# RMS norms that sum their squares as token columns, take the root there and spread it with four products

## The chip, the cores and the metric

The kernel runs on one core of one Trainium2 chip. A core has five engines that run side by side and meet at semaphores: PE (TensorE, matrix products), DVE (VectorE, elementwise), ACT (ScalarE, activation functions), POOL (GpSimd) and SP, which here issues DMAs. PE writes to PSUM only; the other tiles lie in SBUF, with 128 partitions. The metric is the device time of one execution in microseconds (us); lower is better.

## The reference

The program computes two transformer-like blocks on 512 tokens of width 1024 (with a context of 256 tokens, and a memory of 256 tokens), about fifty weight arrays in all, and a final norm. The change touches only the RMS norms over the model width:

```
def _rmsnorm(x, g):
    x32 = x.astype(jnp.float32)
    y = x32 * lax.rsqrt(jnp.mean(x32 * x32, axis=-1, keepdims=True) + EPS)
    return (y * g.astype(jnp.float32)).astype(x.dtype)
```

In the first block the same norm is followed by `modulate`, h * (1 + scale) + shift. The norms of query and key heads and of the gated linear attention are other code and stay as they are. Seven norms go through the changed code, in five stages:

```
h  = modulate(rms_norm(x, norm1_g[l]), shift1, scale1)      # stage 1, 512 tokens
hc = modulate(rms_norm(xc, norm1_g[l]), cmods[0], cmods[1]) # stage 1, 256 tokens, done first
h  = modulate(rms_norm(x, norm2_g[l]), shift2, scale2)      # stage 2, before the experts
mem_n = _rmsnorm(mem, g_mem); h = _rmsnorm(x, g_mix)        # stage 3, 256 and 512 tokens
hm = _rmsnorm(x, g_mlp)                                     # stage 4
return _rmsnorm(x, g_final)                                 # stage 5
```

## The kernel before, in words

Activations lie transposed: the model width is cut into KD = 8 tiles of P = 128 channels, one channel per partition, and the tokens run along the free dimension (n = 512 or 256 columns). The kernel is a row of stages. Each is a block in which every engine has its own list of instructions, written out by hand, and all engines meet at a barrier at the end of the block. So inside a norm stage nothing of the stage before or after runs, except weight loads that were issued earlier (and, in stage 1, the splitting of two weight chunks on ACT and POOL).

A norm stage (`norm_stage`, line 456) takes a list of items. For each item:

- ACT squares the eight tiles into a ring of four buffers `sq` (line 484), and waits for PE to have used a buffer before it is filled again.
- PE adds up over the partitions with a product (line 511). The stationary operand is `K.ones`, 128 x 128; the moving operand is the tile of squares with its n token columns. The eight products accumulate in one bank of PSUM, and since all of `K.ones` is one, every partition of the result holds the same row of n sums.
- DVE makes mean plus EPS out of it (line 530, n columns on every partition), then the reciprocal (line 532).
- ACT takes the root (line 489), n columns on every partition, into `rstd`.
- DVE multiplies each of the eight tiles by its gain column and by `rstd` (line 536). Where the output is split in two parts (`pair`), ACT writes the high part of each tile (lines 494 and 496), and DVE the rest (lines 521 and 523); otherwise ACT adds the shift (line 501), or nothing follows. In stage 5 SP stores each tile when it is scaled.

A float32 product shows in the trace as two records of the matrix product (PE) and two of the weight load (PEld): 16 records for eight products. Other products that are named below are `mod_turn` (line 319, stationary 128 x 128 and two moving columns), the router's (line 259 called from the stage behind stage 2: stationary 128 x 128, 16 moving columns), line 1254 of the gated linear attention (128 x 128 and 128 moving columns) and the transposes of line 2510. All these are float32 too.

Within a stage with two items PE's list is: eight products of the first item, a wait for the first item's mean (`mean_done`), eight products of the second.

Of the kernel before, what the change touches and what calls it, by code (L numbers as in the profile page):

```python
# [10 lines left out]
ACT = mybir.ActivationFunctionType  # L11
AX = mybir.AxisListType

P = 128
D = 1024
KD = D // P
S = 512
# [3 lines left out]
EPS = 1e-6  # L21
# [433 lines left out]

def norm_stage(K, items, tmp, store=None, split=None, first=()):

    sq_done, stored, mean_done, rec_done, rstd_done, scaled, shifted, sq_used, hi_done, lo_done = K.signals(10)
    sq = K.at(tmp, 4, S)
    rec, rstd = K.at(tmp + 8, S), K.at(tmp + 10, S)  # L460
    full = K.at(tmp + 12, KD, S) if any(isinstance(it[2], tuple) for it in items) else None
    with K.nc.Block() as block:
        @block.sync
        def _(sp):
            K.start(sp)
            if store is not None:
                for t in range(KD):
                    sp.wait_ge(scaled, t + 1)
                    sp.dma_start(store[t * P:(t + 1) * P, :], items[0][2][:, t, :]).then_inc(stored, 16)
                sp.wait_ge(stored, 16 * KD)  # L470

        @block.gpsimd
        def _(pool):
            for n in first:
                split.low(K, pool, n)

        @block.scalar
        def _(act):
            for j, (x, n, out, gain, shift) in enumerate(items):
                for t in range(KD):  # L480
                    a = j * KD + t
                    if a >= 4:
                        act.wait_ge(sq_used, a - 3)
                    act.activation(sq[:, a % 4, 0:n], x[:, t, :], ACT.Square).then_inc(sq_done, 1)  # L484
                if j == 0:
                    for c in first:
                        split.high(K, act, c)
                act.wait_ge(rec_done, j + 1)
                act.activation(rstd[:, 0:n], rec[:, 0:n], ACT.Sqrt).then_inc(rstd_done, 1)  # L489
                if isinstance(out, tuple):  # L490
                    for t in range(KD):
                        act.wait_ge(scaled, j * KD + t + 1)
                        if shift is None:
                            ins = act.activation(out[0][:, t, :], full[:, t, :], ACT.Copy)
                        else:
                            ins = act.activation(out[0][:, t, :], full[:, t, :], ACT.Identity, bias=shift(t))
                        ins.then_inc(hi_done, 1)
                elif shift is not None:
                    for t in range(KD):
                        act.wait_ge(scaled, j * KD + t + 1)  # L500
                        act.activation(out[:, t, :], out[:, t, :], ACT.Identity, bias=shift(t)).then_inc(shifted, 1)

        @block.tensor
        def _(pe):
            for j, (x, n, out, gain, shift) in enumerate(items):
                if j >= 1:
                    pe.wait_ge(mean_done, j)
                for t in range(KD):
                    a = j * KD + t
                    pe.wait_ge(sq_done, a + 1)  # L510
                    pe.matmul(K.ps[:, 0, 0:n], K.ones[:, :], sq[:, a % 4, 0:n], start=(t == 0), stop=(t == KD - 1))\  # L511
                        .then_inc(sq_used, 1)

        @block.vector
        def _(dve):
            for j, (x, n, out, gain, shift) in enumerate(items):
                def rest(t):
                    f, hi, lo = full[:, t, :], out[0][:, t, :].bitcast(F32), out[1][:, t, :]
                    dve.wait_ge(hi_done, t + 1)
                    if shift is None:  # L520
                        ins = dve.tensor_tensor(lo, f, hi, ALU.subtract)
                    else:
                        ins = dve.scalar_tensor_tensor(lo, f, shift(t), hi, ALU.add, ALU.subtract)
                    ins.then_inc(lo_done, 1)

                pair = isinstance(out, tuple)
                dve.wait_ge(sq_used, (j + 1) * KD)
                if j >= 1:
                    dve.wait_ge(scaled, j * KD)
                dve.tensor_scalar(rec[:, 0:n], K.ps[:, 0, 0:n], 1.0 / D, EPS, ALU.mult, ALU.add).then_inc(mean_done, 1)  # L530
                dve.wait_ge(mean_done, j + 1)
                dve.reciprocal(rec[:, 0:n], rec[:, 0:n]).then_inc(rec_done, 1)  # L532
                dve.wait_ge(rstd_done, j + 1)
                for t in range(KD):
                    dest = full[:, t, :] if pair else out[:, t, :]
                    dve.scalar_tensor_tensor(dest, x[:, t, :], gain(t), rstd[:, 0:n], ALU.mult, ALU.mult)\  # L536
                        .then_inc(scaled, 1)
                    if pair and t >= 2:
                        rest(t - 2)
                if pair:  # L540
                    rest(KD - 2)
                    rest(KD - 1)
            dve.wait_ge(scaled, len(items) * KD)
# [3175 lines left out]
def block2_stages(K):  # L3719
    K.memT, K.qd, K.kd, K.vd = K.at(72, KD, NCTX), K.at(72, 6, S), K.at(84, 6, S), K.at(96, 12, 256)  # L3720
    K.qm, K.kmT, K.vm = K.at(108, 4, S), K.at(116, 4, NCTX), K.at(120, 2, 512)
    K.rg = K.at(124, 2, 6, P)
    K.hank0, K.hank1, K.hank2 = K.at(124, 4, 256), K.at(128, 4, P), K.at(130, 4, P)
    K.lru_rate, K.flip, K.pick = K.at(132, 6), K.at(132.5, P), K.at(133, 256)[0:4]
    return [
        lambda: load_memory_stage(K),
        lambda: norm_stage(K, [(K.memT, NCTX, K.memT, gain_of(K, "g_mem_2"), None),
                               (K.xT, S, (K.h_hi, K.h_lo), gain_of(K, "g_mix_2"), None)], 80),
        lambda: memory_project_stage(K),
        lambda: lru_weights_stage(K),  # L3730
        lambda: lru_stage(K),
        lambda: dilated_project_stage(K),
    ]
# [16 lines left out]
def mlp_stages(K):  # L3750
    rounded_h(K)
    return [
        lambda: norm_stage(K, [(K.xT, S, (K.h_hi, K.h_lo), gain_of(K, "g_mlp_2"), None)], 128),
        lambda: mlp_stage(K),
    ]


def final_stages(K):
    K.hT = K.at(16, KD, S)
    return [  # L3760
        lambda: norm_stage(K, [(K.xT, S, K.hT, gain_of(K, "g_final_2"), None)], 72, store=K.out),
    ]
# [59 lines left out]
```

## Time and profile before

| | |
|---|---|
| median of 3 runs | 2583.42 us (2577.92 to 2586.68) |
| profiled execution | 2587.65 us, of which the span from first to last instruction is 2585.8 us |
| PE busy | 2220.1 us, 86% of the span |
| DVE busy | 1147.4 us, 44% |
| ACT busy | 866.6 us, 34% |
| mean granted TensorE clock | 0.912 of full speed |

Busy shares are averages over some forty stages with different limits. PE is the busiest engine of the whole, but a stage such as a norm, shut in between two barriers, is as long as its own chain: squares, products, mean, reciprocal, root, scaling. TensorE has two clock levels, 1.2 and 2.4 GHz; PEclk gives the granted one as a share of full speed, 0.50 for 1.2 GHz. In the first 45 us of the trace the column shows 1.00 while the records have the lengths of the lower level, so there lengths are to be read, not that column.

### The profile page before, as it was taken

What the parts mean: (1) busy time and instruction counts of PE and PEld (TensorE: products, weight loads), DVE (VectorE), ACT (ScalarE), POOL (GpSimd) and SP (SyncE); (2) the same over time, 40 slices, a digit from 0 to 9 for tenths busy, and PEclk for the clock granted to TensorE, in tenths of its full rate; (3) what the DMA queues carried; (4) which work ended last, traced back from release to release, by engine and by line L of the source; (5) the groups of instructions that cost most, each with busy time, mean ns of one, the idle gap of its engine ahead of it and who ended that gap; (6) DMA issues with size and microseconds to landing.
All of it is one profiled execution on the core that took longest, in us unless ns stands there. A gap on an engine that the chain in (4) does not pass through costs nothing. (4 is left out here: it accounts for less than half of the span.)

```text
span 2585.8 us, 23825 instructions
## 1 busy us (share of the span) xinstructions
PE 2220.1 (86%) x9452; PEld 1660.4 (64%) x9452; DVE 1147.4 (44%) x1486; ACT 866.6 (34%) x1124; POOL 576.9 (22%) x178
## 2 busy tenths in 40 slices
PE   5789987979888999759999637989779987999997
PEld 2667753547327887657777525678448865788885
DVE  1444357625654123247888543711761232322323
ACT  2441212323212222226777421831532232222221
POOL 0320110022113444010000101333014440544340
PEclk9896888989998999859999868999889998999999
DMA  6213022322004233139999802222012231323210
GB/s 209 88 65 134 24 83 98 131 81 78 0 0 130 74 98 106 49 131 354 376 383 388 316 19 87 98 80 85 11 31 92 90 106 49 130 75 104 81 66 33
DMA packets 174848, 299.69 MB, mean 116 GB/s; under 512 B 8943, under 2 KB 66490, under 8 KB 174744
## 3 DMA queue, kind: packets, MB, share of 16 engines
q1 hardware_dynamic: 169400, 279.93, 31.4%
q0 software_dynamic: 3040, 9.93, 1.1%
q10 hardware_dynamic: 2304, 8.39, 0.8%
q8 instruction: 72, 1.18, 0.2%
q14 instruction: 32, 0.26, 0.0%
HBM read 275.10 MB, written 23.13 MB: 115 GB/s over the span
## 5 line engine op out<-in xcount | busy, mean ns | idle before, releaser
L130 POOL TENSOR_TENSOR region<-weights,region 128x2048 fp32r<-128x2048 f32 (+2 forms) x96 | 378.6, 3945 | 1053.8 <-ACT region L124 917.6
L236 PE MATMUL ps<-region 128*128 128x512 f32 (+1 forms) x1336 | 538.2, 403 | 80.9 <-PEq L2743 16.6
L239 PE MATMUL ps<-region 128*128 128x512 f32 (+1 forms) x1336 | 524.8, 393 | 0.0
L240 PE MATMUL ps<-region 128*128 128x512 f32 (+1 forms) x1336 | 524.3, 392 | 0.0
L236 PEld LDWEIGHTS ps<-region 128*128 128x128 f32 x1336 | 263.1, 197 | 146.4 <-issue 44.7
L239 PEld LDWEIGHTS ps<-region 128*128 128x128 f32 x1336 | 263.0, 197 | 54.8 <-issue 5.4
L240 PEld LDWEIGHTS ps<-region 128*128 128x128 f32 x1336 | 262.1, 196 | 51.1
L124 ACT ACTIVATE region<-weights 128x2048 fp32r<-128x2048 f32 (+2 forms) x98 | 158.4, 1621 | 319.8 <-PE ps L240 278.6
L2584 DVE TENSOR_TENSOR region<-weights,region 128x2048 fp32r<-128x2048 f32 x96 | 218.7, 2290 | 67.0 <-ACT region L2523 66.8
L277 PE MATMUL ps<-region 128*128 128x512 f32 x512 | 203.8, 398 | 24.3 <-POOL region L3353 21.9
L2523 ACT ACTIVATE region<-weights 128x2048 fp32r<-128x2048 f32 x96 | 183.8, 1918 | 84.9 <-DMA weights<-moe_w_up 30.7
L3353 POOL TENSOR_TENSOR region<-weights,region 128x2048 fp32r<-128x2048 f32 x32 | 148.9, 4667 | 233.2 <-ACT region L3414 233.2
L279 PE MATMUL ps<-region 128*128 128x512 f32 x512 | 200.6, 392 | 0.0
L278 PE MATMUL ps<-region 128*128 128x512 f32 x512 | 200.1, 391 | 0.0
L2465 PE MATMUL ps<-region 128*128 128x512 f32 x384 | 154.5, 402 | 10.8 <-issue 8.6
L2195 DVE TENSOR_TENSOR region<-ps,region 128x512 f32<-128x512 f32 x48 | 33.1, 690 | 281.1 <-PE ps L240 281.1
L2467 PE MATMUL ps<-region 128*128 128x512 f32 x384 | 151.6, 395 | 0.0
L2466 PE MATMUL ps<-region 128*128 128x512 f32 x384 | 151.5, 395 | 0.0
L277 PEld LDWEIGHTS ps<-region 128*128 128x128 f32 x512 | 96.7, 189 | 47.6 <-POOL region L3353 22.8
L279 PEld LDWEIGHTS ps<-region 128*128 128x128 f32 x512 | 96.5, 189 | 20.8
L278 PEld LDWEIGHTS ps<-region 128*128 128x128 f32 x512 | 96.9, 189 | 19.3
L3414 ACT ACTIVATE region<-weights 128x2048 fp32r<-128x2048 f32 x32 | 60.1, 1910 | 119.8 <-PE ps L3394 118.4
(375 smaller groups left out, 2801.0 us busy)
## 6 DMA issues: line engine op xcount, KB each, us to landing
weights<-w_in SPq DMA_DIRECT2D x54, 1024.0 KB, 5.1
weights<-moe_w_gate SPq DMA_DIRECT2D x32, 1024.0 KB, 8.0
weights<-moe_w_up SPq DMA_DIRECT2D x32, 1024.0 KB, 8.9
weights<-moe_w_down SPq DMA_DIRECT2D x32, 1024.0 KB, 7.7
weights<-w_mod SPq DMA_DIRECT2D x24, 1024.0 KB, 5.2
weights<-w_mlp_in SPq DMA_DIRECT2D x16, 1024.0 KB, 5.1
weights<-w_mlp_out SPq DMA_DIRECT2D x16, 1024.0 KB, 5.0
h_slots<-region SPq DMA_DIRECT2D x16, 512.0 KB
```

Source lines behind the costliest of these rows:

```text
L124: act.activation(flat(self.part(K, n, 0)), flat(r.view(n)), ACT.Copy).then_inc(self.hi_done, 1)
L130: eng.tensor_tensor(flat(self.part(K, n, 1)), flat(self.ring.view(n)), flat(self.part(K, n, 0)).bitcast(F32), ALU.subtract).then_inc(self. ...
L236: ins = pe.matmul(out, l_hi, r_hi, start=(start and k == 0), stop=False)
L239: pe.matmul(out, l_hi, r_lo, start=False, stop=False)
L240: ins = pe.matmul(out, l_lo, r_hi, start=False, stop=(stop and k == kt - 1))
L277: pe.matmul(out, w_hi, x_hi, start=(n == 0), stop=False)
L278: pe.matmul(out, w_hi, x_lo, start=False, stop=False)
L279: last = pe.matmul(out, w_lo, x_hi, start=False, stop=(n == len(triples) - 1))
L2465: pe.matmul(K.ps[:, bank, :], x_hi[:, x, :], w_hi[:, k, :], start=(start and k == 0), stop=False)
L2467: ins = pe.matmul(K.ps[:, bank, :], x_lo[:, x, :], w_hi[:, k, :], start=False, stop=(stop and k == 3))
L2523: act.activation(flat(part(c, 0)), r.slots[n % RING][:, :], ACT.Copy).then_inc(hi_done, 1)
L2584: dve.tensor_tensor(flat(part(c, 1)), r.slots[n % RING][:, :], flat(part(c, 0)).bitcast(F32), ALU.subtract).then_inc(r.used, 1)
```

## The change

The squares become the stationary operand, a block of 128 tokens at a time, and one column of ones is moved through. The result has tokens on partitions: column c holds the sums of tokens 128c to 128c+127. For 512 tokens that is four products a tile, 32 for an item, in place of eight. Mean, reciprocal and root then work on 128 partitions x 4 columns (2 for 256 tokens). To give every partition the row of roots again, PE multiplies: stationary operand is the root column broadcast to 128 x 128, moving operand the identity, four products of 128 columns into PSUM bank 1 (two for 256 tokens). DVE reads that bank when it scales. `first` and everything else stays.

```
-                act.activation(rstd[:, 0:n], rec[:, 0:n], ACT.Sqrt).then_inc(rstd_done, 1)
+                act.activation(root[:, 0:n // P], rec[:, 0:n // P], ACT.Sqrt).then_inc(root_done, 1)
...
                 for t in range(KD):
                     a = j * KD + t
                     pe.wait_ge(sq_done, a + 1)
-                    pe.matmul(K.ps[:, 0, 0:n], K.ones[:, :], sq[:, a % 4, 0:n], start=(t == 0), stop=(t == KD - 1))\
-                        .then_inc(sq_used, 1)
+                    for c in range(n // P):
+                        ins = pe.matmul(K.ps[:, 0, c:c + 1], sq[:, a % 4, c * P:(c + 1) * P], K.ones[:, 0:1],
+                                        start=(t == 0 and c == 0), stop=(t == KD - 1 and c == n // P - 1))
+                    ins.then_inc(sq_used, 1)
+                pe.wait_ge(root_done, j + 1)
+                if j >= 1:
+                    pe.wait_ge(scaled, j * KD)
+                for c in range(n // P):
+                    ins = pe.matmul(K.ps[:, 1, c * P:(c + 1) * P], root[:, c:c + 1].broadcast_to([P, P]), K.ident[:, :],
+                                    start=True, stop=True)
+                ins.then_inc(rstd_done, 1)
...
-                dve.tensor_scalar(rec[:, 0:n], K.ps[:, 0, 0:n], 1.0 / D, EPS, ALU.mult, ALU.add).then_inc(mean_done, 1)
+                q = n // P
+                dve.tensor_scalar(rec[:, 0:q], K.ps[:, 0, 0:q], 1.0 / D, EPS, ALU.mult, ALU.add).then_inc(mean_done, 1)
                 dve.wait_ge(mean_done, j + 1)
-                dve.reciprocal(rec[:, 0:n], rec[:, 0:n]).then_inc(rec_done, 1)
+                dve.reciprocal(rec[:, 0:q], rec[:, 0:q]).then_inc(rec_done, 1)
                 dve.wait_ge(rstd_done, j + 1)
                 for t in range(KD):
                     dest = full[:, t, :] if pair else out[:, t, :]
-                    dve.scalar_tensor_tensor(dest, x[:, t, :], gain(t), rstd[:, 0:n], ALU.mult, ALU.mult)\
+                    dve.scalar_tensor_tensor(dest, x[:, t, :], gain(t), K.ps[:, 1, 0:n], ALU.mult, ALU.mult)\
```

What PE has in a row in stage 1, before (the branches are the ends and beginnings of blocks; 319 is `mod_turn`, 511 the sums of squares, of the context first and of x behind):

```order
L319 MATMUL ps<-both,region 128x2 x8
L331 UNCONDITIONAL_BRANCH
L503 UNCONDITIONAL_BRANCH
L511 MATMUL ps<-region,ones 128x256 x8
L511 MATMUL ps<-region,ones 128x512 x8
L462 UNCONDITIONAL_BRANCH
```

And now, where line 516 is a sum for 128 tokens and line 523 the spreading of the roots:

```order
L319 MATMUL ps<-both,region 128x2 x8
L331 UNCONDITIONAL_BRANCH
L507 UNCONDITIONAL_BRANCH
L516 MATMUL ps<-ones,region 128x1 x16
L523 MATMUL ps<-ident,region 128x128 x2
L516 MATMUL ps<-ones,region 128x1 x32
L523 MATMUL ps<-ident,region 128x128 x4
L466 UNCONDITIONAL_BRANCH
```

The spreading of the first item now stands ahead of the sums of the second, in PE's own list, and each spreading waits for ACT's root. Stage 3 has the same list; stages 2, 4 and 5 have the last two kinds alone (32 and 4).

DVE's list in stage 3, before (530 is the mean, 532 the reciprocal, 536 the scaling):

```order
L530 TENSOR_SCALAR region<-ps 128x256
L532 RECIPROCAL region<-region 128x256
L536 SCALAR_TENSOR_TENSOR region<-region,vec_cols 128x256 x8
L530 TENSOR_SCALAR region<-ps 128x512
L532 RECIPROCAL region<-region 128x512
```

And now, as lines 544, 546 and 550:

```order
L544 TENSOR_SCALAR region<-ps 128x2
L546 RECIPROCAL region<-region 128x2
L550 SCALAR_TENSOR_TENSOR region<-region,vec_cols,ps 128x256 x8
L544 TENSOR_SCALAR region<-ps 128x4
L546 RECIPROCAL region<-region 128x4
```

DVE's order is the same; the operations between the sums and the scaling are narrow, and the scaling reads PSUM.

## Rows read from the trace of the kernel before

**Rows 1.** Timeline of stage 2: start, length, engine, line, operation, [idle before <-releaser].

```profile
1075.86 8.83 PE L511 MATMUL ps<-region,ones 128*128 128x512 f32 x16 [1.97 <-ACT region L484]
...
1084.73 0.69 DVE L530 TENSOR_SCALAR region<-ps 128x512 f32<-128x512 f32 x1 [10.05 <-PE ps L511]
1085.46 3.35 DVE L532 RECIPROCAL region<-region 128x512 f32<-128x512 f32 x1
1088.85 0.63 ACT L489 ACTIVATE region<-region 128x512 f32<-128x512 f32 x1 [5.62 <-DVE region L532]
1089.51 5.39 DVE L536 SCALAR_TENSOR_TENSOR region<-region,gains 128x512 f32<-128x512 f32 x8 [0.70 <-ACT region L489]
```

**Rows 2.** Timeline of stages 1 and 3, mean to scaling of the 256-token items.

```profile
44.60 0.42 DVE L530 TENSOR_SCALAR region<-ps 128x256 f32<-128x256 f32 x1 [6.61 <-PE ps L511]
...
47.30 3.26 DVE L536 SCALAR_TENSOR_TENSOR region<-region,gains 128x256 f32<-128x256 f32 x8 [0.48 <-ACT region L489]
...
1518.89 3.26 DVE L536 SCALAR_TENSOR_TENSOR region<-region,vec_cols 128x256 f32<-128x256 f32 x8 [0.48 <-ACT region L489]
1519.52 8.80 PE L511 MATMUL ps<-region,ones 128*128 128x512 f32 x16 [3.36 <-ACT region L484]
```

**Rows 3.** Windows over the seven sums: length, busy PE, clock, DMA share, GB/s.

```profile
38.90:44.60 5.70, 5.59 (x16) 1.00 0.17 58
51.70:61.20 9.50, 9.42 (x16) 0.75 0.00 0
1075.80:1084.70 8.90, 8.83 (x16) 0.81 0.00 0
1511.00:1516.20 5.20, 5.16 (x16) 0.72 0.00 0
1519.50:1528.40 8.90, 8.80 (x16) 0.81 0.01 2
2171.60:2180.60 9.00, 8.83 (x16) 0.81 0.00 1
2565.80:2573.10 7.30, 7.13 (x16) 1.00 0.00 1
```

**Rows 4.** Timeline of stage 2, two weight loads of its sums.

```profile
1076.83 0.19 PEld L511 LDWEIGHTS ps<-region,ones 128*128 128x128 f32 x1 [0.24 <-issue]
...
1077.47 0.34 PEld L511 LDWEIGHTS ps<-region,ones 128*128 128x128 f32 x1 [0.45 <-ACT region L484]
```

**Rows 5.** Timeline, the router's products behind stage 2.

```profile
1095.96 13.80 PE L259 MATMUL ps<-router,region 128*128 128x16 f32 x64 [11.26 <-PEq L462]
```

**Rows 6.** Windows, all engines: length, PE, PEld, DVE, ACT, POOL, clock.

```profile
220.00:266.00 46.00, 46.00 (x224) 35.15 (x224) 18.15 (x71) 7.98 (x42) 0.00 (x0) 0.50 0.00 1
1098.00:1102.00 4.00, 4.00 (x21) 4.00 (x20) 0.00 (x0) 0.00 (x0) 0.00 (x0) 0.50 0.00 0
1800.00:1850.00 50.00, 45.10 (x372) 35.26 (x371) 34.15 (x68) 29.13 (x129) 2.43 (x1) 1.00 0.12 38
```

**Rows 7.** Timeline, the transposition of the modulation rows at 422 us.

```profile
422.28 0.97 PEld L319 LDWEIGHTS ps<-both,region 128*128 128x128 f32 x8 [1.21 <-ACT region L431]
422.28 1.05 PE L319 MATMUL ps<-both,region 128*128 128x2 f32 x8 [0.81 <-ACT region L431]
```

**Rows 8.** Groups by line and form: busy us, mean ns of one, idle.

```profile
L441 DVE TENSOR_TENSOR mods<-ps,vec_cols 128x4 f32<-128x4 f32 x8 | 1.2, 152 | 0.0
L2351 DVE RECIPROCAL region<-region 128x4 f32<-128x4 f32 x1 | 0.2, 178 | 0.0
L352 ACT ACTIVATE silu_c<-vec_cols 128x8 f32<-128x8 f32 x1 | 0.2, 199 | 0.0
L2217 DVE SCALAR_TENSOR_TENSOR region<-ps,mods,region 128x512 f32<-128x512 f32 x8 | 6.0, 751 | 33.9 <-PE ps L240 33.9
```

**Rows 9.** Timeline, products of 128 columns.

```profile
219.04 1.22 PE L1254 MATMUL ps<-region 128*128 128x128 f32 x4
...
1484.44 1.97 PE L2510 MATMUL ps<-ident,region 128*128 128x128 f32 x8 [3.44 <-DVE region L2624]
```

More of the change, by code:

```diff
@@ L456, in norm_stage @@
 def norm_stage(K, items, tmp, store=None, split=None, first=()):
-    sq_done, stored, mean_done, rec_done, rstd_done, scaled, shifted, sq_used, hi_done, lo_done = K.signals(10)
+    (sq_done, stored, mean_done, rec_done, rstd_done, scaled, shifted, sq_used, hi_done, lo_done,
+     root_done) = K.signals(11)
     sq = K.at(tmp, 4, S)
-    rec, rstd = K.at(tmp + 8, S), K.at(tmp + 10, S)
+    rec, root = K.at(tmp + 8, S), K.at(tmp + 10, S)
     full = K.at(tmp + 12, KD, S) if any(isinstance(it[2], tuple) for it in items) else None
```

## The prediction

> **What bounds the norms now.** I read the timeline of the norm stages first, then the windows over their sums, then the groups of narrow operations. Stage 2 shows the shape of all of them [rows 1]: PE adds the squares for 8.83 us, DVE waits 10.05 us for that, and then mean, reciprocal and root follow one another. From the start of the mean (1084.73) to the start of the scaling (1089.51) it is 4.78 us, of which the reciprocal has 3.35. No other stage can run beside this, so every microsecond of this chain is a microsecond of the kernel. The five items of 512 tokens all have the 4.78. The two of 256 tokens have 2.70 (44.60 to 47.30) [rows 2].
>
> The windows show the sums themselves [rows 3]: 16 records each (eight float32 products), 9.42, 8.83, 8.80, 8.83 and 7.13 us for 512 tokens, 5.59 and 5.16 us for 256 (the first of these began at the low clock too, whatever its column says, in the part of the trace where that column stands at 1.00). The same work takes different times because TensorE's clock differs: granted 1.00 all through in stage 5 (7.13 us), 0.75 on average in stage 1, 0.81 in stages 2, 3 and 4. In stage 2 the clock was full at first and fell after a pause of 1.97 us and 1.3 us of products: a weight load took 0.19 us at 1076.83 and 0.34 us at 1077.47 [rows 1, 4]. It came back within the sums, while PE streamed 512 columns a record.
>
> **The sums, part by part.** An item of 512 tokens has 32 products now, 64 records, each with its own 128 x 128 load and one moving column. The nearest rows are two. The router's 32 products have the same loads and 16 moving columns: 64 records in 13.80 us [rows 5], about 0.213 us a record, at a granted clock of 0.50, 1.2 GHz [rows 6]. The turning of the modulation rows has two moving columns: eight loads in 0.97 us, that is (0.97 - 0.19) / 7 = 0.111 us a record, half of the router's, so this is 2.4 GHz [rows 4, 7]. At either clock the load sets the pace, not the columns. An item of 64 records then takes 13.8 us at the low level and 64 x 0.111 + 0.1 = 7.2 us at the high one; one of 32 records half, 6.9 and 3.6 us. Before, it was 7.13 at the high level. So at one clock old and new cost the same, and the whole question of the sums is the clock that they get.
>
> I take the low one, since the nearest stretch decides: the router's products keep PE without a gap for 13.80 us and the clock stays at 0.50 in them [rows 5, 6]. Even 46 us of float32 products with up to 128 moving columns, PE never idle, stayed at 0.50 [rows 6] (window 220 to 266). One column is less than either. What an item that arrives at the full clock does is not shown; in stage 2 the old one fell 1.3 us in [rows 4], and I let the new one fall there too, and not come back.
>
> - Stage 1, context: 6.9 - 5.59 = +1.3. Stage 1, x: 13.8 - 9.42 = +4.4; it begins at the low clock.
> - Stage 2: 13 records at 0.111 (1.4 us), 51 at 0.213 (10.9 us), 0.4 us for the last to drain: 12.7 - 8.83 = +3.9. Stage 4 likewise, +3.9.
> - Stage 3, memory: 6.9 - 5.16 = +1.7. Then x, which before found the full clock that the memory's sums had won and now does not: 13.8 - 8.80 = +5.0.
> - Stage 5 did not fall before. Never falling gives 7.2, falling as in stage 2 gives 12.7; I take a fall after 3 us, 3.0 + 37 x 0.213 + 0.4 = 11.3, less 7.13 = +4.2.
>
> Sum of the sums: +24.4 us. If every record ran at the low level it would be 5 x 13.8 + 2 x 6.9 = 82.8 against 53.8 before, +29.0; with every clock as it was, near zero.
>
> **From the sums to the scaling.** Mean on 128 x 4 out of PSUM: a like operation took 0.152 us [rows 8], with 0.04 us between two of DVE's as in [rows 1] 0.20. Reciprocal on 128 x 4: 0.178 [rows 8], 0.21 with its gap. Root on 128 x 4: 0.199 for 128 x 8 on ACT [rows 8], 0.27 with the hops to ACT and to PE. Then the added wait and four spreading products, eight records: transposes of the same shape took 1.97 us for eight from a standing start at the low clock [rows 9], 0.04 us to DVE. Together 2.69 us for 4.78: -2.1 us, five times, -10.5. At the full clock eight records took 1.05 us [rows 7], so the chain would be 1.8 and the gain 3.0. For 256 tokens four records take 1.22 [rows 9] and some 0.1 for the standing start: 2.0 against 2.70, -0.7 twice, -1.4. These gains do not depend on the operations being hidden, since nothing hid the old ones.
>
> Behind the wait for the root stand, in PE's list, the sums of a second item. In stage 1 those squares come later anyway, as ACT first adds shifts. In stage 3 ACT squares while PE spreads, so the sums may begin when the scaling begins, where before they began 0.6 us after it (1518.89, 1519.52) [rows 2]: -0.6. ACT's four buffers are freed more slowly, but PE, not ACT, is what ends last in either kernel. The scaling reads PSUM in place of a tile in SBUF: a like operation out of PSUM took 0.751 us, and the eight old ones 5.39 us together, 0.67 a step where they overlap at their ends, [rows 1, 8]. I put the difference at 0, between -0.5 and +1 us in all. The stage behind begins at the low clock in either kernel, PE having been idle at least for the scaling, 5.39 us [rows 1]: 0. Sum behind the sums: -12.5 us.
>
> **Total.** +24.4 - 12.5 = +11.9 us. The profiled execution took 2587.65 us (span 2585.8 and 1.85 around it) and would take 2599.6. It lies 4.2 above the median of the three runs, 2583.42, against which the forecast is 2595.3. With each bound at its worst (+29.0, gains 12.5, scaling +1) it is +17.5, 2601; with the clock of stages 2, 4 and 5 falling 1.6 us later than I let it, 1.6 x (0.213 / 0.111 - 1) = 1.5 us less in each, +7.4, 2591.
>
> **Rivals.**
> - *The clock rises, or holds, as it did.* Sums +0.3 each (0.111 x 8 = 0.89 a tile for 0.86), +2; chain at the full clock 5 x -3.0 = -15.0, the two short ones (four records in 0.6) -1.4 each, -0.6 for the overlap. Total -16, 2567. For it: PE is without a gap in the sums, and 45 of 50 us from 1800 on ran at 1.00 with small products in plenty [rows 6]. Against it: the router [rows 5, 6]. The Trainium skill ("TensorE: Matmul & The Clock Gate", "Why this matters for your kernels") tells the author to keep TensorE busy without idle gaps to get the full clock; taken by busy time alone, that gives this rival, and the trace disagrees for columns as few as the router's. [...]
> - *A full clock is not given up.* Items that arrive at the full clock (stages 2, 4, 5) keep it, the others are at the low one. Their sums take 7.2: -1.6, -1.6 and +0.1 in place of +3.9, +3.9 and +4.2, 15.1 less, and their spreading 0.9 less each. Total 11.9 - 15.1 - 2.7 = -5.9, 2577.5. For it: the window at 1800 to 1850. Against it: the clock fell in stage 2 even with wide products behind the pause [rows 4].
> - *Dearer than forecast.* The stage behind each norm gets its full clock later, because PE comes to it from one-column products and not from wide ones. An item that starts at the low clock took 9.42 where one at the full clock took 7.13 [rows 3], so 2.3 us each time at most. Four stages follow a norm: up to +9, 2604. Against it: PE already pauses long before each.
>
> **Chances.** Forecast 0.60, clock as before 0.14, full clock kept 0.14, dearer 0.12. A measurement of this kernel tells about 0.3% from no change, 7.75 us: 2575.7 and 2591.2. Faster: all of the first rival, a third of the second, 0.19. Same: the rest of the second and the low edge of the forecast (a late fall in several stages), 0.09 + 0.14 = 0.23. Slower: 0.58. The forecast's own range is 2589 to 2601. For 8 in 10 it is carried down over the second rival to 2575 and up to 2604; outside lie the first rival and what is beyond the last one.
>
> **What would show it.** Right: PEclk near 0.50 in all sums (stage 5 mixed), 64 records in 12 to 14 us, loads 0.33 us long; 2.5 to 2.9 us from mean to scaling, 1.9 to 2.1 of it the eight spreading records; DVE's scaling steps still 0.67. Wrong in the first way: loads of 0.19 us in the sums and 7 to 9 us an item. Wrong in a way that none of this holds: records further apart than 0.213 us at 0.50, so that load and product don't overlap with squares as the stationary operand, or a spreading that takes over 3 us.

## The result, and the profile after

| | before | after |
|---|---|---|
| median of 7 runs | 2582.22 us (2577.92 to 2586.68) | 2593.97 us (2591.77 to 2602.21) |
| profiled execution | 2587.65 us | 2593.83 us |
| span | 2585.8 us | 2592.0 us |
| PE busy | 2220.1 us | 2256.2 us |
| DVE busy | 1147.4 us | 1124.3 us |

The changed kernel is slower: 1.005 times the time before, 95% interval 1.0036 to 1.0064, which is 11.8 us at the medians and 9.3 to 16.5 us by the interval. The profiled executions differ by 6.2 us only; stages that the change does not touch took 5.7 us less in the one after, as told below.

The rows that answer to [rows 1] are these, from the timeline of the kernel after in stage 2 (start, length, engine, line, operation, count, idle before and releaser):

```profile
1077.67 12.06 PE L516 MATMUL ps<-ones,region 128*128 128x1 f32 x64 [1.97 <-ACT region L488]
...
1089.77 0.16 DVE L544 TENSOR_SCALAR region<-ps 128x4 f32<-128x4 f32 x1 [13.28 <-PE ps L516]
1089.96 0.18 DVE L546 RECIPROCAL region<-region 128x4 f32<-128x4 f32 x1
1090.17 0.20 ACT L493 ACTIVATE region<-region 128x4 f32<-128x4 f32 x1 [5.31 <-DVE region L546]
1090.43 1.78 PEld L523 LDWEIGHTS ps<-ident,region 128*128 128x128 f32 x8 [0.79 <-ACT region L493]
1090.43 2.08 PE L523 MATMUL ps<-ident,region 128*128 128x128 f32 x8 [0.70 <-ACT region L493]
1092.55 5.36 DVE L550 SCALAR_TENSOR_TENSOR region<-region,gains,ps 128x512 f32<-128x512 f32 x8 [2.41 <-PE ps L523]
```

The narrow operations are as short as they look: from the mean to the root's end is 0.60 us where the wide ones took 4.75. The spreading then takes 2.08 us, so the scaling starts 2.78 us after the mean, against 4.78. But the sums ahead take 12.06 us where they took 8.83.

The windows over PE's sums say why; they answer to [rows 3] (window, its length, PE busy and records, granted clock, DMA share, GB/s):

```profile
38.80:45.90 7.10, 6.99 (x32) 1.00 0.14 45
52.20:66.10 13.90, 13.78 (x64) 1.00 0.00 0
1077.70:1089.80 12.10, 12.03 (x64) 0.58 0.00 0
1508.30:1515.40 7.10, 6.99 (x32) 0.50 0.01 2
1517.20:1530.70 13.50, 13.46 (x65) 0.50 0.00 0
2170.00:2183.50 13.50, 12.75 (x64) 0.57 0.00 1
2567.20:2581.30 14.10, 13.61 (x64) 0.52 0.01 2
```

The granted clock is 0.50 to 0.58 in every window from stage 2 on, where it was 0.72 to 1.00. In stage 1 the column still shows 1.00, but 64 records take 13.78 us there, the length that they have at 0.50 elsewhere. The weight loads show the moment of the fall in stage 2, in narrow windows of the timeline: three loads span 0.41 us (0.11 apart), and 1.6 us later two span 0.55 (0.22 apart). It did not come back before the end of the sums: 17 records 0.111 us apart and 47 at the low clock's 0.213 make up the 12 us.

```profile
1078.33 0.41 PEld L516 LDWEIGHTS ps<-ones,region 128*128 128x128 f32 x3
...
1079.92 0.55 PEld L516 LDWEIGHTS ps<-ones,region 128*128 128x128 f32 x2
```

From the start of the first square to the first record of PE in the next stage (in stage 5, to the end of the span), read from the two timelines:

| | before | after | difference | forecast |
|---|---|---|---|---|
| stage 1 | 38.52 | 41.46 | +2.9 | +2.9 |
| stage 2 | 20.78 | 21.98 | +1.2 | +1.8 |
| stage 3 | 33.27 | 36.28 | +3.0 | +3.3 |
| stage 4 | 31.44 | 33.34 | +1.9 | +1.8 |
| stage 5 | 20.60 | 25.10 | +4.5 | +2.1 |
| together | | | +13.6 | +11.9 |

Of the +13.6 us the seven sums make +26.1 (79.8 us in place of 53.8); what lies behind them makes -12.5.

The long stages of the experts, between the router's first product and the first square of stage 3, took 414.6 us in the profile before and 408.9 in the one after; in the profiles of the first four experiments, which leave them alone too, they took 409.3 to 413.6. They vary by some 5 us from one execution to the next. That hides part of the norms' loss in the profiled pair, and may well be why the profiled execution before lies 5.4 us over its median.

### The profile page after: what moved, and what is told of

Read it like the earlier page. It is cut to its first block and busy times, and to the rows that moved or that the text cites. A ratio compares the mean times of both kernels' runs of the same rounds, so it can differ in the third digit from the quotient of the medians.

```text
span 2592.0 us, 24467 instructions
## 1 busy us (share of the span) xinstructions
PE 2256.2 (87%) x9772; PEld 1722.4 (66%) x9772; DVE 1124.3 (43%) x1486; ACT 864.9 (33%) x1124; POOL 578.8 (22%) x178
## 5 line engine op out<-in xcount | busy, mean ns | idle before, releaser
L2479 PE MATMUL ps<-region 128*128 128x512 f32 x384 | 154.2, 402 | 11.3 <-issue 7.0
```

Of the source, the lines that this page charges most:

```text
L2479: pe.matmul(K.ps[:, bank, :], x_hi[:, x, :], w_hi[:, k, :], start=(start and k == 0), stop=False)
```

## The experiments

**One part undone: the old sums in front of the new chain.** The four narrow columns are here sums of tokens 0 to 3, so this kernel leaves out the per-token roots and is for timing only.

```
-                    for c in range(n // P):
-                        ins = pe.matmul(K.ps[:, 0, c:c + 1], sq[:, a % 4, c * P:(c + 1) * P], K.ones[:, 0:1],
-                                        start=(t == 0 and c == 0), stop=(t == KD - 1 and c == n // P - 1))
+                    ins = pe.matmul(K.ps[:, 0, 0:n], K.ones[:, :], sq[:, a % 4, 0:n], start=(t == 0), stop=(t == KD - 1))
```

> The changed kernel with one part undone: the sums are again eight products of 512 (256) columns with K.ones stationary; mean, reciprocal and root stay narrow and the four spreading products stay. It leaves out part of the computation: the four columns that the narrow operations take are the sums of tokens 0 to 3, so the roots are not those of the reference and only the time counts. Theory (the clock takes the gain): sums at 7.1 to 9.4 us an item with the clock coming back within them, as before; mean to scaling 1.8 to 2.8 us in place of 4.78; so 12 to 17 us faster than the kernel before, about 2568 us, and some 26 us under the changed kernel. Rival (the new chain or its added wait costs, not the sums): no faster than 5 us under the kernel before.

2564.41 us, 0.9922 of the kernel before (0.9900 to 0.9944), 18.7 us under it and a little more than expected. Its timeline in stage 2:

```profile
1070.91 8.83 PE L515 MATMUL ps<-region,ones 128*128 128x512 f32 x16 [1.97 <-ACT region L488]
...
1079.78 0.16 DVE L542 TENSOR_SCALAR region<-ps 128x4 f32<-128x4 f32 x1 [10.05 <-PE ps L515]
...
1080.45 1.16 PE L521 MATMUL ps<-ident,region 128*128 128x128 f32 x8 [0.70 <-ACT region L493]
1081.64 5.36 DVE L548 SCALAR_TENSOR_TENSOR region<-region,gains,ps 128x512 f32<-128x512 f32 x8 [1.49 <-PE ps L521]
```

The sums are back at 8.83 us, to the hundredth what they were in this stage; the seven together take 52.5 us in place of 53.8, since the item of 512 tokens in stage 3 runs at the full clock here (7.11 us in place of 8.80). And the chain behind is shorter than in the changed kernel, 1.86 us against 2.78, since the spreading too finds the full clock (1.16 us for eight records against 2.08). Leaving out the 1.3 us of the sums, the new chain is worth some 17 us where its spreading finds the full clock; the one-column sums cost all of the gain and 12 us more, 29.6 us between the two versions.

**More columns through the same loads.** `W` was 128, 64 and 16 in place of one; the narrow mean reads the first column of each group.

```
-                        ins = pe.matmul(K.ps[:, 0, c:c + 1], sq[:, a % 4, c * P:(c + 1) * P], K.ones[:, 0:1],
+                        ins = pe.matmul(K.ps[:, 0, c * P:c * P + W], sq[:, a % 4, c * P:(c + 1) * P], K.ones[:, 0:W],
...
-                dve.tensor_scalar(rec[:, 0:q], K.ps[:, 0, 0:q], 1.0 / D, EPS, ALU.mult, ALU.add).then_inc(mean_done, 1)
+                sums = K.ps[:, 0, 0:n].rearrange("p (c k) -> p c k", k=P)[:, :, 0]
+                dve.tensor_scalar(rec[:, 0:q], sums, 1.0 / D, EPS, ALU.mult, ALU.add).then_inc(mean_done, 1)
```

> The changed kernel with 128 moving columns of ones in place of one in each sum; the first column of each 128 is read. Loads, number of products and everything else stay. Theory (the clock depends on how much the array streams, and one column is too little): the clock comes back within the sums, loads go from 0.33 to 0.19 us, an item of 512 tokens takes 7 to 10 us instead of 12 to 14, and the whole is 10 to 17 us under the changed kernel, near 2580 or below. Rival (products of 128 columns or fewer with a load each never bring the clock back, as in the window from 220 to 266 us of the kernel before): granted clock 0.50, 0.213 us a record, time the same as the changed kernel within 0.1%, 2594.

2569.73 us, 0.9949 of the kernel before (0.9935 to 0.9963), and 24 us under the changed kernel. PE streams 128 times as many columns, in the same 64 records an item, and is faster. The windows over the five 512-token sums, 128 columns:

```profile
49.80:59.80 10.00, 9.85 (x64) 0.74 0.00 0
1070.90:1080.00 9.10, 9.04 (x64) 0.81 0.00 0
1505.20:1512.70 7.50, 7.39 (x65) 1.00 0.00 0
2153.00:2162.10 9.10, 9.04 (x64) 0.81 0.00 1
2544.10:2551.70 7.60, 7.41 (x64) 1.00 0.01 3
```

The clock is the one of the old sums [rows 3], 0.74 to 1.00, and the lengths are the old ones to within some 0.4 us, 7.41 against 7.13 us in stage 5 (the item of stage 3 is shorter by 1.4, as the clock holds all through it here). The gain was larger than the 10 to 17 us expected. The sums alone are some 26 us shorter than in the changed kernel, for which the expected lengths of an item (7 to 10 us in place of 12 to 14) had left room. The spreading finds the full clock as well: in stage 2 the scaling starts 1.86 us after the mean, some 5 us in all.

> As with 128 columns, but 64 moving columns: half of what the load's time would allow. Theory (share of streaming decides): between the two, either full clock in part of the sums or 0.50 throughout; if the 128 columns bring the clock back and these do not, the limit lies between them. Rival: 0.213 us a record, 0.50, 2594.

2589.17 us, one run. The windows over the same five items with 64 columns:

```profile
51.00:65.00 14.00, 13.88 (x64) 0.50 0.00 0
1076.40:1088.70 12.30, 12.13 (x64) 0.58 0.00 0
1517.90:1531.80 13.90, 13.82 (x66) 0.50 0.00 0
2173.00:2186.10 13.10, 12.97 (x64) 0.54 0.00 1
2570.00:2577.50 7.50, 7.36 (x64) 1.00 0.01 3
```

The first four items are as in the changed kernel. The last, in stage 5, arrived at the full clock and kept it for all of its 7.36 us. That is the second rival of the prediction seen in one item; what decides between this item and those of stages 2 and 4, which arrive the same way and fall, these runs do not show.

> As with 128 columns, but 16 moving columns, the router's number. Both theories: granted clock 0.50 in the sums, 64 records in 12 to 14 us, 2594 us, like the changed kernel; anything under 2588 would say that the router's low clock has another cause.

2595.9 us, one run: the changed kernel again. Its windows in stages 2 and 5:

```profile
1076.00:1088.10 12.10, 12.04 (x64) 0.58 0.00 0
2569.50:2583.30 13.80, 13.76 (x64) 0.50 0.01 2
```

**The suspected cost doubled.**

```
                     for c in range(n // P):
+                        pe.matmul(K.ps[:, 2, c:c + 1], sq[:, a % 4, c * P:(c + 1) * P], K.ones[:, 0:1],
+                                  start=(t == 0 and c == 0), stop=(t == KD - 1 and c == n // P - 1))
+                    for c in range(n // P):
                         ins = pe.matmul(K.ps[:, 0, c:c + 1], sq[:, a % 4, c * P:(c + 1) * P], K.ones[:, 0:1],
```

> The changed kernel with each one-column sum product issued twice, the extra ones into an unused bank of PSUM. Theory (PE's records in the sums are all on the path and run at the low clock): 0.213 us for each of the added 384 records, +82 us less what the items that arrive at the full clock take at it, near 2674 us, granted clock 0.50 in the sums. Rival (PE's records are in part hidden behind ACT's squares or the semaphores, or the clock comes back if PE is busy long enough): under +60 us, and with the clock back near +45.

2679.52 us, one run: 85.6 us over the changed kernel for 384 more records, where 82 were expected. The five norm stages, measured as in the table above, are 80.7 us longer, 0.210 us a record; the rest lies in stages that the edit does not touch. In stage 2, 128 records took 24.43 us at 0.56:

```profile
1097.50:1122.00 24.50, 24.43 (x128) 0.56 0.00 1
```

So PE without a gap for 24 us did not win the full clock with one-column products, and each of their records is paid in full, at the low clock's price.

**Half the records.** The 128-column version and the kernel before, both with squares and ones rounded by ACT (`fp32r`), so that a product is one record. The lines that both edits share (the product then takes `ones` in place of `K.ones`):

```
-    sq = K.at(tmp, 4, S)
+    sq = K.rounded_at(32, 4, S)
...
+    ones = K.rounded_at(41, P)
...
+                    if a == 0:
+                        act.activation(ones, K.ones[:, :], ACT.Copy).then_inc(ones_done, 1)
```

> The 128-column version with the squares and the ones written by ACT in the rounded float32 format, so that a product has one record and one load instead of two. Stage 5's free memory is cut into regions differently for that. Theory (PE's records bound the sums): 32 records an item; at 0.111 to 0.213 us each 3.6 to 6.9 us, but ACT's eight squares take 4.3 (0.52 a step), so 4.5 to 7 us an item instead of 7 to 10; 10 to 15 us under the 128-column version, near 2556. Rival (fewer records are less work for the array, the clock then stays low, 0.213 us a record): 6.9 us an item, only 5 to 8 us under it, near 2563.

2566.31 us, 0.9935 of the kernel before (0.9911 to 0.9959): 3.4 us under the 128-column version, less than the theory (10 to 15) and the rival (5 to 8) said, and with overlapping intervals. For a record the rival's number holds. Stage 2's sums:

```profile
1072.35 6.33 PE L520 MATMUL ps<-region 128*128 128x128 f32 x32 [2.26 <-ACT region L491]
```

32 records in 6.33 us; in stages 1 and 3 it was 7.06 and 7.07, some 0.22 each, the low clock's pace. Only stage 5 had 4.21 us. The spreading is at the low clock too, 2.08 us in stages 1 to 4, where the 128-column version had 1.16; neither expectation counted that.

> The kernel before with rounded squares and ones: eight records of 512 columns an item, 0.225 us each at the full clock and 0.43 at the low one, and the wide mean, reciprocal and root as they were. Theory: the sums are bound by ACT's squares, about 4.8 to 5.2 us an item of 512 tokens instead of 7.1 to 9.4; the 4.78 us behind them stay; 15 to 20 us under the kernel before, near 2565, and 5 to 12 us above the rounded version with token columns, if the narrow chain is worth its spreading also when the sums are cheap. Rival: the two rounded versions are within 3 us, the short chain being eaten by the slower loads.

2560.26 us, 0.9896 of the kernel before (0.9867 to 0.9926), 23.6 us under it where 15 to 20 were expected, and the lowest median of all versions measured here. Its timeline in stage 2:

```profile
1069.05 4.34 PE L515 MATMUL ps<-region 128*128 128x512 f32 x8 [2.26 <-ACT region L487]
1073.44 0.69 DVE L534 TENSOR_SCALAR region<-ps 128x512 f32<-128x512 f32 x1 [5.86 <-PE ps L515]
1074.16 3.35 DVE L536 RECIPROCAL region<-region 128x512 f32<-128x512 f32 x1
...
1078.21 5.39 DVE L540 SCALAR_TENSOR_TENSOR region<-region,gains 128x512 f32<-128x512 f32 x8 [0.70 <-ACT region L492]
```

With eight rounded records the sums take 4.34 us in stages 2, 3 and 4, which is ACT's pace for eight squares; what PE's clock is no longer matters much: stages 1 and 5 have 4.16 and 4.05 us. The wide chain of 4.78 us is all kept. The expectation that token columns would be 5 to 12 us faster than this fell: the loads that they need, 32 against 8, cost at the low clock what the short chain saves. In the profiles the norm stages 2, 3 and 4 are alike to 0.2 us; stage 1 is 1.8 us shorter in the old form, and stage 5, where the token columns had the full clock, 2.8 us shorter in the new one. The rival said within 3 us; the medians are 6 apart with the old form ahead and the intervals overlap, so which of the two rounded forms is faster is not settled, only that the token columns have no lead.

## Why the prediction was right

The forecast was +11.9 us and 2595.3; measured were +11.8 and 2593.97. The mechanism was right: the sums pay for the low clock more than the short chain saves. That the two numbers agree to 0.1 us is luck. The interval goes from 9.3 to 16.5 us, and in the profiled pair the norm stages lost 13.6: +26.1 in the sums against a forecast of +24.4, and -12.5 behind them, as forecast. Point by point:

- *At one clock the old and new sums cost the same.* Right as far as it was measured. With 128 columns, at the clock that the old sums had, 9.04 us stand against 8.83 in stages 2 and 4, and at the full clock 7.41 against 7.13. At the low clock the new sums took 13.78 us, the router's 13.8; no old item ran at it from end to end.
- *The one-column sums get the low clock.* Right, and the cause of the loss: undoing them alone turns 1.005 into 0.9922, and more columns through the same loads give 0.9949. PE's busy time does not make the difference: the stretch of 24.43 us was as busy as any. Of the two supports that the prediction gave, only the router's held. The 46 us at 0.50 from 220 on were put as products of up to 128 columns, and with 128 columns the clock came back here. The groups of that window, in the kernel before, show another mixture (line, operation, shapes, count, busy us and mean ns, in that window): 58 of its 224 records have a full 128 x 128 load, the others half or a quarter of one. Whether that makes the difference was not tested.

```profile
L1254 PE MATMUL ps<-region 128*128 128x128 f32 x58 | 17.7, 460 | 0.0
L1260 PE MATMUL ps<-region 64*64 64x128 f32 x114 | 16.1, 432 | 0.0
L1241 PE MATMUL ps<-region 64*128 64x128 f32 x52 | 15.8, 457 | 0.0
```

- *An item of 512 tokens takes 13.8 from a low start, 12.7 where it arrives at the full clock.* 13.78, and 12.06 and 12.75: the clock fell later than I let it in stage 2.
- *Stage 5 at 11.3 us.* Too small. It took 13.61: the clock fell at once there, two loads at 2567.97 already spanning 0.55 us. This was a guess between 7.2 and 12.7 and the measured value lies outside it, at +6.5 instead of +4.2. It is the largest miss of a term, 2.3 us; the 64-column run, with 7.36 us in the same place, shows how far the term can move.
- *The chain.* 2.69 us forecast, 2.78 measured; the spreading had 2.08 in place of 1.97 and all the rest was within 0.05. For 256 tokens 1.91 (45.86 to 47.77) in place of 2.0.
- *The sums of stage 3's second item begin when the scaling of the first does.* They begin 0.24 us ahead of it (1517.01, 1517.25), so the gain there was 0.9 and not 0.6.
- *The scaling reads PSUM at no cost.* Right: eight take 5.36 us against 5.39.
- *The stage behind does not suffer.* Right. Stage 1's follower begins with a record of 0.77 us, as before, so at the low clock in either kernel; and the four stretches between the norm stages took 997.2, 408.9, 625.9 and 363.5 us where they took 998.2, 414.6, 627.2 and 362.8.
- *Rivals.* The first (the clock as it was) is what the 128-column version is, and its forecast of 2567 stands beside a measured 2569.73. The Trainium skill's advice ("TensorE: Matmul & The Clock Gate", "Why this matters for your kernels") to keep TensorE busy without gaps, taken by busy time alone, would have put the changed kernel there; the 24.43 us at 0.56 contradict it for one-column products, as the router's row did ahead. The second was seen in one item of one variant. The third, up to 2.3 us more behind each norm, did not occur: none of the four stretches grew by more than 0.7 us.

The chance for "slower", 0.58, was modest. What made it so was the clock, which no row showed for one column: taking the router's 16 columns for it was a judgement, and the run with 16 columns, 2595.9 us, shows that it was a good one.

## What to carry to other kernels

A float32 product with a 128 x 128 load and a few moving columns costs its load (0.111 us a record at the full clock, 0.213 at the low one), so making the data stationary to get a narrow result does not save PE time; and it can lose the clock: here the same records took 12 to 14 us with one moving column and 7 to 10 with 128, the other 127 results being thrown away. Before a chain behind a product is shortened by changing the product, ask at which granted clock the new product will run, and take that from a stretch of the trace with about as few columns. And look for what paces the product itself: with rounded operands the old form was bound by the squares at either clock, and its 2560.26 us beat the 2569.73 of the best version with float32 token columns, long chain and all.

## What the runs showed that was not expected

- A product that streams more can be faster: one column 2593.97 us, 16 columns 2595.9, 64 columns 2589.17, 128 columns 2569.73, with the same loads. Those with 16 and 64 columns are single runs.
- The clock that an item meets in stage 5 varies from version to version: 64 records took 13.61 us with one column, 13.76 with 16, 7.36 with 64. Each of these is one trace; whether the next execution of the same version would meet the same clock there is not shown.
- The experts' stages take 409 to 415 us from one profile to the next with nothing changed in them, which is half of the effect measured here. Two profiled executions would have put it at 6.2 us, where the medians say 11.8.
